# One gather lane over all token blocks, with separate u and v rings, mixers and searches woven beside it, and part of the v rows added on VectorE

## What is computed

```
h = x @ w_in
A = forgetting attention (8 heads, causal, with the log forget gates summed along the keys)
B = differential attention (4 heads of two maps each, chunk-causal, relative bias)
x = LayerNorm(alpha*x + concat(A, B) @ w_out)

q  = x @ w_pq ; s, i = top_k(scores against 2 x 128 sub-keys, 16)      (8 heads)
top, sel = top_k(all 256 sums, 16) ; g = softmax(top)                  (8 x 16 = 128 experts per frame)
a  = g * gelu(x . u_tab[expert])
x  = LayerNorm(alpha*x + sum over the 128 experts of a * v_tab[expert])
```

## Time and profile before

| | |
|---|---|
| median of the runs | 2119.59 us |
| profiled execution, span | 2113.0 us |
| bytes moved | 759.05 MB, 359 GB/s over the span |
| busy: PE, DVE, ACT, POOL | 1847.5, 1189.1, 694.1, 1293.6 us |

### The profile page before, as it was taken

One profiled execution on the slowest core, in us unless ns is written; L12 is line 12 of the kernel. 1 busy time (PEld: TensorE's weight loads), 2 busy tenths in 40 slices (PEclk: granted clock), 3 DMA queues, 4 the chain that ended last, 5 costly groups with the idle time before them and its releaser, 6 DMA issues.

```text
span 2113.0 us, 25770 instructions
## 1 busy us (share of the span) xinstructions
PE 1847.5 (87%) x7056; PEld 1048.4 (50%) x7056; DVE 1189.1 (56%) x2936; ACT 694.1 (33%) x1925; POOL 1293.6 (61%) x1198
## 2 busy tenths in 40 slices
PE   6795999999879999998798999987999998986776
PEld 5564544446445444455464454553655554552332
DVE  2349444557864445478645354787434454797543
ACT  1301324632222246322222464222245663222221
POOL 2004774766667756666577566666446675667774
PEclk9897999999989999999899999999999999998989
DMA  9457999999999999999999999999979999999996
GB/s 344 170 183 287 408 408 383 339 360 399 404 347 399 408 391 330 360 392 399 345 400 408 392 328 360 390 400 347 368 287 353 373 398 387 345 366 344 396 408 264
DMA packets 213316, 759.05 MB, mean 359 GB/s; under 512 B 24400, under 2 KB 28792, under 8 KB 212904
## 3 DMA queue, kind: packets, MB, share of 16 engines
q0 software_dynamic: 167168, 612.07, 75.6%
q1 hardware_dynamic: 45992, 145.17, 18.1%
HBM read 747.14 MB, written 13.28 MB: 360 GB/s over the span
## 4 chain that ended last, share of the span: by engine, by line
PE 60%; DMA 17%; DVE 10%; issue 6%; ACT 4%; POOL 3%; DVEq 0%; POOLq 0%; ACTq 0%; SPq 0%; PEldq 0%
PE acc L629 34%; DMA vbuf<-in_peer_v,idx_cur 13%; PE ps_o L610 4%; PE ps_o L434 4%; DVE ubuf L1006 3%; PE ps_o L569 3%; PE ps_o L550 3%; PE ps_s L493 3%; DMA wring<-in_w_qk 2%; PE ps_t L513 2%; POOL ubuf L1049 2%; PE ps_o L461 2%; PE ps_s L497 1%; DMA ubuf<-in_peer_u,idx_cur 1%; ACT L675 1%
## 5 line engine op out<-in xcount | busy, mean ns | idle before, releaser
L629 PE MATMUL acc<-vbuf,diag 128*128 128x512 f32 x2304 | 1060.3, 612 | 118.1 <-DMA vbuf<-in_peer_v,idx_cur 98.6
L1049 POOL DMA_INDIRECT ubuf<-in_peer_u,idx_cur x576 | 663.3, 1152 | 394.7 <-DVE hid L1006 234.3
L629 PEld LDWEIGHTS acc<-vbuf,diag 128*128 128x128 f32 x2304 | 436.9, 196 | 673.0 <-issue 629.5
L1006 DVE CUSTOM_DVE_ANT_0 ubuf<-ubuf,x_cur 128x1024 f32<-128x1024 f32 x576 | 677.2, 1222 | 159.9 <-DMA ubuf<-in_peer_u,idx_cur 137.9
L1049 POOL DMA_INDIRECT vbuf<-in_peer_v,idx_cur x576 | 610.3, 1060 | 232.5 <-issue 154.1
L747 ACT ACTIVATE diag<-ident,coef 128x128 f32<-128x128 f32 x576 | 193.1, 392 | 153.8 <-PE acc L629 141.5
L434 PE MATMUL ps_o<-xT,wring 128*128 128x128 f32 x1280 | 170.9, 299 | 62.5 <-DMA wring<-in_w_qk 30.4
L434 PEld LDWEIGHTS ps_o<-xT,wring 128*128 128x128 f32 x1280 | 167.3, 214 | 76.8 <-issue 29.3
L832 DVE CUSTOM_DVE_ANT_0 region<-ps_s,region 128x512 f32<-128x512 f32 (+2 forms) x80 | 59.5, 744 | 235.8 <-PE ps_s L497 151.9
L610 PEld LDWEIGHTS ps_o<-region,wring 128*128 128x128 f32 x1280 | 151.3, 195 | 18.4 <-issue 16.6
L610 PE MATMUL ps_o<-region,wring 128*128 128x128 f32 x1280 | 152.7, 279 | 3.9 <-ACT region L710 3.9
(11 more groups left out here) (169 smaller groups left out, 1399.8 us busy)
## 6 DMA issues: line engine op xcount, KB each, us to landing
wring<-in_w_qk SPq DMA_DIRECT2D x80, 512.0 KB, 7.6
wring<-in_w_pq SPq DMA_DIRECT2D x80, 512.0 KB, 7.2
wring<-in_w_out SPq DMA_DIRECT2D x40, 512.0 KB, 7.2
wring<-in_w_v SPq DMA_DIRECT2D x20, 512.0 KB, 8.4
ubuf<-in_peer_u,idx_cur POOLq DMA_INDIRECT x576, 7.8
vbuf<-in_peer_v,idx_cur POOLq DMA_INDIRECT x576, 8.5
region<-scr_tpl SPq DMA_DIRECT2D x4, 1280.0 KB, 16.7
wring<-in_c_k SPq DMA_DIRECT2D x8, 512.0 KB, 7.4
```

What stands on the lines that cost most here:

```text
L629: last = pe.matmul(acc[:, hf * 512:(hf + 1) * 512], diag[:, j, :], vbuf[:, j, hf * 512:(hf + 1) * 512], start=first_slot, stop=last_slot)
L1006: nc.vector.tensor_tensor_reduce(out=ubuf[:, j, :], in0=ubuf[:, j, :], in1=x1_cur[:, :], scale=1.0, scalar=0.0, op0=ALU.mult, op1=ALU.add, ...
L1049: pool.indirect_dma_start(buf[:, j, :], None, a[table], bass.IndirectOffsetOnAxis(ap=idx_cur[:, at:at + 1], axis=0)).then_inc(landed_[j], 16)
```

## The change

- **Lanes.** Five kinds of generators per engine: `x` (projections and gates of a block), `y` (attention to key scores), `t` (search), `j` (the gather lane: one step per slot over all 576 slots), `f` and `n` (second LayerNorm). `spans()` gives each lane of each block a stretch on the axis of gather steps, and `weave()` issues the steps of all lanes by their marks, on each engine alike. All loops are unrolled.
- **Gather lane.** Step j gathers u row j and v row j-4; VectorE handles u row j-3; ScalarE and TensorE v row j-7. It doesn't stop between blocks: x is kept in three tiles, numbers and weights g in two.
- **Rings.** `ubuf` 6, `vbuf` 6, `diag` 4; `hid`, `act_h`, `coef` 16 columns. `wring` 6.
- **v rows on VectorE.** `on_tensor(k)` is false for 97 of the 576 rows (24, 25, 25, 23 and 0 in the five blocks): these VectorE adds into `y_acc` (L1119), which ScalarE has set to alpha*x. The coefficients are now one VectorE multiply per four slots (L1108).
- **Attention** takes only the keys there are: 128, 256, 384, 512 for the prompt blocks. ScalarE scales 12 of 16 head outputs.
- **Scores** are made for four tiles at once and copied by ScalarE to `sc`, from which the search reads. The numbers are decoded in two halves of 4 heads (before 4, 3, 1).
- **Opening.** The bias table is built once in `bias_p` (no store to memory, no reload per block). `held` is loaded behind the sixteen q and k tiles.

```diff
-WRING = 4
-RING = 8
+WRING = 6
+URING, VRING = 6, 6
+U_LAG = 3
+V_AT = GRP
+V_LAG = U_LAG + GRP
+def on_tensor(k):
+    p = part_of(k)
+    at = k - p * SLOTS
+    if p == SMP:
+        return True
+    if at < 3:
+        return False
+    lo, hi = (52, 116) if p == SMP - 1 else (62, 122)
+    return lo <= at < hi or k % 3 != 2
+        if p == 0:
+            x, y, t = (-100.0, -70.0), (-70.0, -30.0), (-34.5, 4.0)
+        elif p == SMP:
+            x, y, t = (334.0, 366.0), (368.0, 440.0), (436.5, 500.0)
+        else:
+            b = (p - 1) * SLOTS
+            x, y, t = (b - 30.0, b + 8.0), (b + 14.0, b + 72.0), (b + 66.5, b + 121.0)
...
-            with pool.Fori(0, NBP) as i:
-                gpsimd_block(pool, i, SETS, False)
-            gpsimd_block(pool, NBP, SSETS, True)
+            for j in range(JSLOTS + V_AT):
+                if j < JSLOTS:
+                    gather(pool, "peer_u", j)
+                if j >= V_AT:
+                    gather(pool, "peer_v", j - V_AT)
...
-            nc.vector.scalar_tensor_tensor(y_sb[:, :], x1_cur[:, :], ALPHA, acc[:, :], ALU.mult, ALU.add).then_inc(acc_read, 1)
+                v = j - V_LAG
+                if v >= 0 and not on_tensor(v):
...
+                    nc.vector.scalar_tensor_tensor(y_acc[p % 2][:, :], vbuf[:, v % VRING, :], coef[:, v % MARKS:v % MARKS + 1],
+                                                   y_acc[p % 2][:, :], ALU.mult, ALU.add).then_inc(vD_used, 1)
```

More of the change, by code:

```diff
@@ L75 @@
[L75 to L80, removed]
+SETUP_ROWS = 4
+FCH = FLEN // SETUP_ROWS
+SMP = NBP
+LAST = NB - 1
+WRING = 6
+HELD = 4
+X_STEPS, Y_STEPS = 12, 28
+T_PLAN = [("round", r, s) for r in range(6) for s in range(4)] + [("decode", 0, s) for s in range(5)]
+T_PLAN += [("round", r, s) for r in range(6, HEADS + 1) for s in range(4)] + [("decode", 1, s) for s in range(5)]
@@ new lines, with nkeys, rounds_of, spans @@
+PE_COUNT = [0]
+for _k in range(JSLOTS):
+    PE_COUNT.append(PE_COUNT[-1] + on_tensor(_k))
+def nkeys(p):
+    return SKEYS if p == SMP else (p + 1) * P
+def rounds_of(p):
+    t = nkeys(p) // P
+    return [(c, min(4, t - c)) for c in range(0, t, 4)]
+T_ROUNDS = [MATS * len(rounds_of(p)) + 4 for p in range(NB)]
+T_BASE = [sum(T_ROUNDS[:p]) for p in range(NB + 1)]
+def spans():
+    out = [("j", 0, J_STEPS, 0.0, float(J_STEPS))]
+    for p in range(NB):
+        if p == 0:
[5 more added lines that the diff above has]
+            x, y, t = (b - 30.0, b + 8.0), (b + 14.0, b + 72.0), (b + 66.5, b + 121.0)
+        out += [("x", p, X_STEPS) + x, ("y", p, Y_STEPS) + y, ("t", p, T_STEPS) + t]
+        end = float(min((p + 1) * SLOTS, JSLOTS) + V_LAG)
+        out.append(("f", p, 1, end + 1.0, end + 2.0))
+        rows = 445.0 if p == SMP - 2 else end + 4.0
+        out.append(("n", p, 2, rows, rows + 4.0))
+    return out
@@ new lines, in weave, with x_tiles @@
+def weave(lanes):
+    marks = []
+    for name, p, steps, lo, hi in spans():
+        marks += [(lo + (k + 0.5) * (hi - lo) / steps, name, p) for k in range(steps)]
+    live = {}
+    for _, name, p in sorted(marks):
+        if name in lanes:
+            if (name, p) not in live:
+                live[name, p] = lanes[name](p)
+            next(live[name, p])
+    for lane in live.values():
+        assert next(lane, None) is None
+def x_tiles(p):
+    return [("qk", i) for i in range(MATS)] + [("wv", i) for i in range(HELD, 8)]
@@ L955, in numbers @@
-            def numbers(c0_, c1):
-                for r, c in ((slice(0, DEC), 0), (slice(DEC, P), DEC)) if sample else ((slice(0, P), c0_),):
-                    last = nc.vector.scalar_tensor_tensor(idx_next[r, c0_:c1], rowid[r, 0, c:c + c1 - c0_], float(NKEYS),
-                                                          rowid[r, 1, c:c + c1 - c0_], ALU.mult, ALU.add)
-                last.then_inc(idx_done, 1)
-            for h in range(HEADS):
-                best(h, h - 1 if h else None)
-                if h == PICK:
-                    rows_of(0, PICK)
-                    if not sample:
-                        wait(dve, idx_taken, b)
-                        numbers(0, PICK * TOPK)
-                if h == HEADS - 1:
-                    rows_of(PICK, HEADS - 1)
-                yield
@@ new lines, in f_vector @@
+        def f_vector(dve, p, chain):
+            link, y, n = chain.link, y_acc[p % 2], p % 2
+            end = min((p + 1) * SLOTS, JSLOTS)
+            dve.wait_ge(vP_used, PE_COUNT[end])
+            wait(dve, vD_used, end - PE_COUNT[end])
+            if p == SMP:
+                dve.wait_ge(acc_made, NB)
+            nc.vector.tensor_tensor(y[:, :], y[:, :], acc[:, :], ALU.add).then_inc(acc_read, 1)
+            dve.wait_ge(acc_read, p + 1)
+            for hf in range(2):
+                last = nc.vector.bn_stats(stats2[:, n, hf, :], y[:, hf * 512:(hf + 1) * 512])
+            link(last)
+            nc.vector.bn_aggr(mv2[:, n, :], stats2[:, n, :, :].rearrange("p a n -> p (a n)")).then_inc(ln2_v, 1)
+            yield
```

1476 lines of the change are left out of this document (743 added, 733 removed).

## The result

The changed kernel takes **2255.89 us** (median of 4 runs, 2246.94 to 2259.87). The kernel before, on the same chip, takes 2120.65. The ratio is 1.063, with an interval of 1.060 to 1.065: slower by 6%, 135 us. Forecast were 2055 us and a range of 1985 to 2125. The profiled execution has a span of 2245.1 us.

The account below looks back on a forecast made before the run. Transfers at 408 GB/s were taken as nearly the bound, GpSimd hardly less. First u product 217, lane 1805 and end 26 gave a 2048 us span; the median stands 6.6 above: 2055 us, range 1985 to 2125.

Parts of the forecast that it names:

- 146 slots with nothing or a prompt attention beside them: Gather lane beside prompt attentions and in gaps: transfers, GpSimd and TensorE bounds nearly equal, 2.65 us per slot, 387 us.
- The projections: Gather lane beside the projections of blocks 2, 3 and the sample block: 120 us each for two, 110 for sample, 350 together.
- the search: Gather lane beside the search: 112 slots at 2.75 us, 308 us, with VectorE at 2.45 us per slot.
- output projections: Gather lane beside output projection and LayerNorm: 41 us of transfers plus 5 of waits; 3 x 46 + 50 = 188 us.
- query projections: Gather lane beside the query projections: TensorE 47 us against 44 for transfers; 3 x 47 + 54 = 195 us.
- Sample attention: 46 slots beside the sample block's attention: TensorE's work 178 us, taken as 190 with short pieces and waits.
- TensorE's 1630 us: TensorE's total busy time falls from 1847 to about 1630 us, through 97 fewer v rows and shorter keys.
- the opening: Start to first u product: 217 us, 17 later than before; search from 134.5, 14 lost waiting for block 1's gates.
- R3: Rival, 10%: engines wait between lanes in mixer norm and merge, 15 us more per block, 2115 us, no change.
- R1: Rival, 14%: locks with VectorE make GpSimd the bound in slots without weights, 2.95 us each, 95 more: 2150 us.
- R2: Rival, 14%: bytes alone bind the lane, twelve buffers covering all waits: 1958 us, up to 2000 with the sample attention.
- The rule weighed: VectorE instructions with two SBUF inputs and GpSimd gathers lock each other out; 97 new adds could cost GpSimd 58 us.

Follow-up runs that it names:

- e4_shift: The changed kernel with the prompt blocks' lane y 0.9 slots later on VectorE and 1.4 later on ScalarE than on TensorE: 2147.08 us, ratio 1.013.
- e8_all: e4_shift plus v rows two slots later, the sample block's heads staggered, and block 1's projections and gates behind the first search: 2076.05 us, ratio 0.976.
- e6_sample: e4_shift with the sample block staggered too: VectorE's step 1.0 slot later, ScalarE's exponentials in their own lane 1.4 later: 2116.08 us, ratio 0.996.
- e2_all_pe: The changed kernel with all v rows on TensorE but the first three of each prompt block: 2320.82 us, ratio 1.095.
- e1_lag: The changed kernel with the v row two slots later, rings unchanged: 2215.28 us, ratio 1.045.
- e5_shift_lag: e4_shift with the v row two slots further behind the u row: 2123.22 us, ratio 1.000.
- e3_table: The changed kernel with exp in place of gelu in the gather lane, removing 89 of 127 table loads: 2199.9 us, ratio 1.038.

## Why the prediction was wrong, step by step

- **The step that failed** is "146 slots with nothing or a prompt attention beside them", "each priced by its bound", 2.65 us. For the 35 gaps it held (85 against 86.1). For the 111 slots with a prompt attention it gave 294 us and they took 407.3. A price by the largest of several bounds supposes that the engines overlap; that had to be read from the order of each engine's instructions, and the order of `weave()` puts a head's dependent parts side by side. e4_shift, with the same instructions in another order, took 313.7. A row of the kernel before warned of it (VectorE by line, 636 to 1060 us): even there the 16 logits of a pass waited 28.7 us for scores, 1.8 us each, where it became 4.1:

```profile
L832 DVE CUSTOM_DVE_ANT_0 region<-ps_s,region 128x512 f32<-128x512 f32 x16 | 11.1, 692 | 40.5 <-PE ps_s L497 26.2 <-issue 11.8 <-PE ps_s L493 2.5
```

- **Once the lanes are staggered the same price is nearly right:** 315.5 us in e8_all against 294; and over all, the span is 2082.6 against 2048. The projections remain 19 us above their term, the search 6. What they wait for there was not tried. In the changed kernel the projections, output projections and query projections stood 58 us above their terms in all; for this part of the miss the cause stays open.
- **Sample attention,** 190 by TensorE's work: it took 213.7. Not a wrong amount of work but the same chain; e6_sample brought it to 189.7.
- **Not varied:** the rings went from 8 buffers to 6, and those of the diagonals from 8 to 4. Their share in the loss is not known; the repaired kernel has the same rings.
- **TensorE's 1630 us:** 479 v rows took 1000.0 us, 2.09 each, where the earlier trace rows gave 1.85: 114 of the 132 us that were missing. The sum took TensorE's time per row for a constant, and two things move it. One is the granted clock, 0.921 over the span and 0.955 in the kernel before: v rows ran 200 us at the lower level, where the kernel before had 69 for its 576 rows, 57 for 479, and half of the difference is some 70 us. The other is that rows come alone or in twos now: at the higher level one alone shows as 1.98 us, four in a row as 7.03, 1.76 each. The other 18 us are the attention itself, whose four lines took 294.5 us before and 273.5 now, 21 less where 39 was written. (The attention of block 0 had 128 keys in the kernel before too, and took 22.8 us there, not 51; "512 keys whatever the block" holds for blocks 1 to 3 alone.)
- **Right:** the opening (217 against 217.87: the search began at 141.6 where 134.5 was written, 7 us later, and its wait for block 1's gates was 11.81 us where 14 were written, so that part of the fit is luck; the rest of the search with gates and copies took 64.4 where 68 were written), the search, the last slots, the bytes. VectorE in time in the changed kernel, the start of the search, the wait for the gates and the first product, which answer to the earlier trace rows:

```profile
141.62 0.49 DVE L1005 MAX8 top_v<-sc 128x8 f32<-128x128 f32 x2 [21.63 <-ACT sc L789]
...
159.93 0.34 DVE L852 TENSOR_SCALAR stage<-ps_t,gbias 8x128 f32<-8x128 f32 x1 [11.81 <-PE ps_t L474]
...
217.87 1.22 DVE L1095 CUSTOM_DVE_ANT_0 ubuf<-ubuf,x 128x1024 f32<-128x1024 f32 x1
```

- **R3, waits between lanes,** had the right kind of mechanism, at the wrong place (norm and merge) and far too small: 15 us per block, where each attention alone lost 24 to 47. Its sign that was to be looked for, "waits of VectorE on TensorE in the mixers of blocks 1 to 3", is the wait of L923.
- **R1, slower by locks,** ended on the right side for the wrong reason. Its own sign (a mean above 1.15 us, GpSimd never idle) doesn't appear: the gathers' mean is 1.08 us and GpSimd is busy 55% in the attentions.
- **R2, bytes alone:** its sign was 400 GB/s throughout. Six of the 40 slices of the changed kernel are above 400, three of them in the last stretch.
- **The rule weighed.** The 58 us estimated for the adds do not appear. In the changed kernel 93 gathers begin during an add of L1119; they take 1.34 us in the mean against 0.94 at rest, which would be 37 us of GpSimd. But all 1152 gathers together take 1246.2 us, 163 above 0.94 each, and in e2_all_pe, with 12 adds in place of 97, they take 1244.2, 161 above. In the kernel before, with no such add, it is 191. So 85 adds more cost GpSimd 2 us in the sum. The Trainium skill, page "SBUF — State Buffer", section "Who interferes with whom", says the same of two-input VectorE instructions as the prediction does; the trace agrees with the rule for a single gather: one that begins in an add ends 0.81 us after the add's end in the median, and one that begins in a u product as long after the product's. One input in PSUM is enough to be out of it: in the kernel before 23 gathers begin in the logits of L832, which read `ps_s`, and take 0.94 us.

## What to carry to other kernels

- When lanes are woven by marks, a consumer on another engine should stand later in the order than its producer. Here 0.9 of a slot on VectorE and 0.9 or 1.4 on ScalarE served; nothing between 0 and 0.9, and nothing above 1.4, was tried. In order, a wait of 4 us for one small tile holds everything behind it, on all engines in turn. Look for windows in which no resource is full; such a window can't be priced by its bounds.
- A wait on TensorE cost twice here: the wait, and the lower clock of the work behind it (28.5 and 15.5 us in one attention).
- Before giving up a restructuring that lost, stagger it: here the same instructions went from 6% slower to 2% faster.

## What was not expected of the hardware

The last 75 slots are bound by GpSimd and the transfers at once, and how fast they run depends on where a gather begins relative to a u product. The changed kernel's 150 gathers of that stretch (2027 to 2220 us) by group:

```profile
L1163 POOL DMA_INDIRECT ubuf<-in_peer_u,idx x75 | 77.3, 1031 | 22.8 <-issue 22.8
L1163 POOL DMA_INDIRECT vbuf<-in_peer_v,idx x75 | 71.2, 949 | 22.8 <-issue 21.9 <-PE acc L668 0.9
```

and those of e1_lag (1980 to 2185 us), with its window:

```profile
L1163 POOL DMA_INDIRECT vbuf<-in_peer_v,idx x75 | 84.5, 1127 | 22.9 <-issue 17.1 <-PE acc L668 5.8
L1163 POOL DMA_INDIRECT ubuf<-in_peer_u,idx x75 | 75.6, 1008 | 22.9 <-issue 22.9
```

```profile
1980.00:2185.00 205.00, 147.27 (x295) 52.80 (x293) 104.33 (x181) 30.70 (x95) 159.56 (x150) 0.97 1.00 382
```

In both GpSimd is never idle but for 0.30 us before a gather: 147.4 + 45.6 = 193.0 and 159.6 + 45.8 = 205.4 us, the length of the stretch each time. In the first, 72 of the u gathers begin during a u product, but with only 0.17 us of it left in the median, and only 5 v gathers do. In the second 45 v gathers begin during one, and these take 1.25 us in the mean. GpSimd and VectorE in time, e1_lag:

```profile
2050.02 1.89 POOL L1163 DMA_INDIRECT vbuf<-in_peer_v,idx  x1 [0.30 <-issue]
```

```profile
2049.89 1.22 DVE L1095 CUSTOM_DVE_ANT_0 ubuf<-ubuf,x 128x1024 f32<-128x1024 f32 x1
```

All v gathers of the stretch take 1.13 us in the mean, this one 1.89; the rate falls from 408 to 382 GB/s. That is R1's mechanism after all, 12 us of it, at one place. In the profiles of the other versions (e5_shift_lag left out) the same stretch took 206.6 us in e3_table and 193 to 202 elsewhere, so these are not two fixed speeds. What sets the phase was not tried.
